# Where the softmax transposes, scores and value sums of two attentions stand between the weight products

## The reference, cut to what matters

```python
s = einsum('bgrqm', q, k) * SCALE - slopes * dist      # selected and window keys, 8 heads each
p = masked_softmax(s, mask)
o = einsum(p, v)
o_nsa = g[0] * o_cmp + g[1] * o_slc + g[2] * o_win     # o_cmp: 15 compressed keys
mixed = sigmoid(gate_a) * (o_nsa @ w_branch_a) + sigmoid(gate_b) * (z @ w_branch_b)
```

```python
s = einsum('bqhd,bqkhd->bhqk', q, k_sel) * HEAD_DIM_2 ** -0.5
out = einsum(softmax(where(valid, s, -inf)), v_sel)
```

## The kernel before, in words

| step | engine | work |
|---|---|---|
| a | TensorE | scores of both rows, 64-row operands in two halves of the array (`TT`), below S |
| a+1 to a+4 | VectorE, ScalarE | `biased`, `exps`, `factors`, `scale_p` (in `SM`; ScalarE at a+4) |
| a+4, a+5 | TensorE | three transposes of row 2n, then of 2n+1 (`turn`, line 433, into the one bank PB[6]), below T |
| a+5, a+6 | ScalarE | `copy_p` of each to `PT` |
| a+6 | TensorE | sums of values of both rows, 64-column outputs (`PT`,`QKV`), below V, and every second time those of the compressed keys (`PTC`,`KCV`), below C |
| a+7 | ScalarE, VectorE | every second time `make_o_hi`, `make_o_lo`, which free PB[7] |

## Time and profile before

### The profile page before, as it was taken

The page is one execution under the profiler, slowest core; times in us unless marked ns, Lnnn a source line. Parts: engine busy times, 40 slices in busy tenths (PEclk is TensorE's granted clock), DMA queues, the critical chain, the costliest instruction groups (busy, mean ns, idle before and its releaser), DMA issues.

```text
span 929.4 us, 14094 instructions
## 1 busy us (share of the span) xinstructions
PE 918.4 (99%) x5341; PEld 787.6 (85%) x5341; DVE 684.9 (74%) x1205; ACT 523.9 (56%) x899; POOL 15.2 (2%) x20
## 2 busy tenths in 40 slices
PE   8999999999999999999999999999999999999997
PEld 6899887788888888888899988888788888888886
DVE  5779976378776666678688989998786676666665
ACT  6656677745654544456544436654946664445443
POOL 0300000000000000000000000000000000000000
PEclk9999999999999999999999999999999999999999
DMA  9845454655565555554655844555475256655551
GB/s 334 307 146 159 137 150 127 237 200 186 166 207 196 193 193 189 193 190 147 206 173 151 235 134 154 172 175 178 138 236 176 93 163 219 217 189 182 181 182 46
DMA packets 89458, 168.54 MB, mean 181 GB/s; under 512 B 7536, under 2 KB 11952, under 8 KB 89136
## 3 DMA queue, kind: packets, MB, share of 16 engines
q1 hardware_dynamic: 89024, 167.13, 55.5%
q10 hardware_dynamic: 368, 0.52, 0.2%
HBM read 164.77 MB, written 1.05 MB: 178 GB/s over the span
## 4 chain that ended last, share of the span: by engine, by line
PE 94%; DVE 3%; issue 1%; DMA 1%; ACT 1%; SPq 0%; POOLq 0%; POOL 0%; DVEq 0%
PE pb L429 92%; PE pb L433 2%; DVE YC L1987 1%; DVE wlo L1527 1%; DMA raw<-in_w_in 1%; ACT whi L976 0%; DVE DG L1966 0%; DVE ST L1677 0%; DVE XS L2261 0%; ACT S L1461 0%; DVE SM L1672 0%; SPq L367 0%; DVE X L2254 0%; DVE ST L2209 0%; ACT SM L976 0%
## 5 line engine op out<-in xcount | busy, mean ns | idle before, releaser
L1527 DVE TENSOR_TENSOR wlo<-raw,whi 128x1024 fp32r<-128x1024 f32 (+2 forms) x300 | 356.0, 1212 | 118.0 <-ACT whi L976 117.4
L976 ACT ACTIVATE whi<-raw 128x1024 fp32r<-128x1024 f32 (+2 forms) x302 | 308.7, 1044 | 134.3 <-PE pb L429 122.2
L429 PE MATMUL pb<-XT,whi 128*128 128x256 f32 (+2 forms) x1424 | 311.1, 334 | 0.8 <-issue 0.8
L429 PEld LDWEIGHTS pb<-XT,whi 128*128 128x128 f32 (+1 forms) x1424 | 234.9, 190 | 23.7 <-issue 4.0
L429 PE MATMUL pb<-whi,ZO 128*128 128x512 f32 (+1 forms) x808 | 252.4, 389 | 0.0
L429 PE MATMUL pb<-XT,wlo 128*128 128x256 f32 (+1 forms) x1032 | 205.5, 282 | 0.0
L429 PE MATMUL pb<-whi,XT 128*128 128x512 f32 (+1 forms) x544 | 176.3, 395 | 2.3 <-ACT whi L976 2.3
L429 PEld LDWEIGHTS pb<-whi,ZO 128*128 128x128 f32 x808 | 151.3, 188 | 31.6 <-DVE wlo L1527 1.1
L429 PEld LDWEIGHTS pb<-XT,wlo 128*128 128x128 f32 (+1 forms) x1032 | 166.8, 190 | 9.6
L429 PE MATMUL pb<-wlo,ZO 128*128 128x512 f32 (+1 forms) x404 | 156.6, 388 | 0.0
L429 PEld LDWEIGHTS pb<-whi,XT 128*128 128x128 f32 x544 | 101.8, 189 | 23.9 <-ACT whi L976 2.8
(11 more groups left out here) (238 smaller groups left out, 593.2 us busy)
## 6 DMA issues: line engine op xcount, KB each, us to landing
raw<-in_w_in SPq DMA_DIRECT2D x107, 512.0 KB, 3.8
raw<-in_w_ff SPq DMA_DIRECT2D x64, 512.0 KB, 4.7
raw<-in_w_up SPq DMA_DIRECT2D x32, 512.0 KB, 4.5
raw<-in_w_down SPq DMA_DIRECT2D x32, 512.0 KB, 5.1
raw<-in_w_branch_b SPq DMA_DIRECT2D x8, 512.0 KB, 4.8
raw<-in_w_out SPq DMA_DIRECT2D x8, 512.0 KB, 4.7
raw<-in_wx_kv SPq DMA_DIRECT2D x8, 512.0 KB, 5.2
raw<-in_w_attn_out SPq DMA_DIRECT2D x8, 512.0 KB, 3.4
```

The lines of the kernel that those rows point to most:

```text
L429: return e.matmul(o, l, r, start=start, stop=stop, skip_group_check=True)
L976: return e.activation(o, i, ACT.Copy, scale=scale)
L1527: e.tensor_tensor(wlo[u % NW][:, 0:c], raw[u % NRAW][:, 0:c], whi[u % NW][:, 0:c].bitcast(F32), ALU.subtract).then_inc(lo, 1)
```

## The change

In the first attention the transposes of row 2n stand at a+3 and those of row 2n+1 at a+6 (a+5 for the last pair); the values of a pair stand at a+9 (a+8 for n = 6, a+6 for n = 7). Since `pair_at` goes in threes, gap s in `pair_at` now holds, in this order: T of the odd row of pair n-2, S of pair n, V of pair n-3, T of the even row of pair n-1. ScalarE's copies stand at the transposes' step +2 (even rows) and +1 (odd rows); `scale_p` stays at a+4. In the second attention the values of a head move from gap 29+2h to 30+2h, behind the scores and the transposes there.

```diff
+        values_of = {a + (9 if i < 6 else 8 if i == 6 else 6): i for i, a in enumerate(pair_at)}
+        def turn_step(j):
+            return pair_at[j // 2] + (3, 6 if j < 14 else 5)[j % 2]
...
+                    def turn_item(j):
+                        e.wait_ge(sc_p, j + 1)
+                        if j:
+                            e.wait_ge(pt_out, j)
+                        for c in range(3):
+                            i = turn(PB[6][:, c * P:c * P + P], SM[j % 4][:, c * P:c * P + P])
+                        i.then_inc(pt_done, 1)
+                    for j in range(1, 16, 2):
+                        if s == turn_step(j):
+                            turn_item(j)
                     if s in pair_of:
...
-                    for p in range(2):
-                        if s - 4 - p in pair_of:
...
-                    if s - 6 in pair_of:
-                        n = pair_of[s - 6]
+                    if s in values_of:
+                        n = values_of[s]
...
+                    for j in range(0, 16, 2):
+                        if s == turn_step(j):
+                            turn_item(j)
                     yield
...
-                    h = (s - 29) // 2
-                    if s % 2 == 1 and 0 <= h < 8:
+                    h = (s - 30) // 2
+                    if s % 2 == 0 and 0 <= h < 8:
                         e.wait_ge(pt_out, 16 + h + 1)
...
-                    for p in range(2):
-                        if s - 5 - p in pair_of:
-                            copy_p(2 * pair_of[s - 5 - p] + p, 0)
-                    if s - 7 in pair_of and pair_of[s - 7] % 2:
-                        f = pair_of[s - 7] // 2
+                    for j in range(16):
+                        if s == turn_step(j) + (2, 1)[j % 2]:
+                            copy_p(j, 0)
+                    if s - 1 in values_of and values_of[s - 1] % 2:
+                        f = values_of[s - 1] // 2
                         make_o_hi(f, 7, (pair_done, f + 1))
```

More of the change, by code:

```diff
@@ L1249, in attention2 @@
             def attention2():
-                for s in range(45):
+                for s in range(46):
                     if s == 1:
@@ L1266, in attention2 @@
                         copy_p((s - 29) // 2, 16)
-                    h = (s - 30) // 2
-                    if s % 2 == 0 and 0 <= h < 8:
+                    h = (s - 31) // 2
+                    if s % 2 == 1 and 0 <= h < 8:
                         make_o_hi(h, 6, (pv_done, 16 + h + 1))
```

## The result

| | runs | median us | range |
|---|---|---|---|
| before | 22 | 929.76 | 928.66 to 931.23 |
| changed | 22 | 931.10 | 930.51 to 931.62 |

The ratio is 1.0015 with a 95% interval of 1.0009 to 1.0021: the change costs 1.34 us, between 0.8 and 2.0. The forecast was 932.1, so 2.2 us; the direction was right and the size about six tenths of it. The result lies in the stated range of 929.9 to 933.4, but outside the forecast's own range of 931.6 to 932.9, and inside the 0.2% that I called about what a measurement can tell. In some sets a few executions are 1 to 1.7 us longer than the rest, most of them at a mean granted clock of 0.996 or 0.997 against 0.998 to 1.000, so the ratios, which are computed from all runs, can differ a little from the quotient of the medians.

The account below looks back on a forecast made before the run. TensorE was taken as the bound, busy 918.4 of 929.4 us. Losses of 1.55 + 0.36 + 0.27 = 2.18 us on 929.91 gave 932.1 us, own range 931.6 to 932.9, whole range 929.9 to 933.4.

Parts of the forecast that it names:

- The wait in gap 31: First attention, end of ga1: row 12's transposes wait for ScalarE's copies and scaling, 1.55 us slower.
- Row 1's hidden place: First attention: row 1's transposes leave gap 15, where a wait hid them, for gap 16, +0.36 us.
- everything up to the end of x1 is free: TensorE's work between gap 13 and the product after x1's bank wait costs nothing, even if row 0 waits.
- The lost pairing: First attention: values follow scores in five gaps instead of six, +0.27 us.
- Gap 28: One gap after ga0's end: row 10's transposes come about even with ScalarE; 0 taken, 0.2 us no surprise.
- The joining: Both attentions: side work stands in 22 gaps fewer, taken as worth 0 us.
- leaving and re-entering the weight products has a price: Rival: the product recorded 0.50 instead of 0.39 is real time, saved 22 times, 2.4 us; 929.7, chance 0.17.
- the 0.2% line: Whole kernel: slower by over 0.2% means above 931.8 us, chance 0.62; within 0.33, faster 0.05.
- my cases: Whole kernel: forecast 0.52, no gap 31 wait 0.12, price of returns 0.17, both 0.04, dearer transposes and more waits 0.15.

Follow-up runs that it names:

- e6_both_mended: Changed kernel with row 12's transposes in gap 32 and row 1's in gap 15; median 929.24 us, 0.9997 times the kernel before.
- e1_row12_later: Changed kernel with row 12's transposes alone in gap 32 instead of ending gap 31; median 929.55 us, 1.0001 times the kernel before.
- e4_first_only: Kernel before with only the first attention's part of the change; median 931.37 us, 1.0018 times the kernel before.

## Why the forecast came out as it did

**The wait in gap 31** was forecast as 1.55 us and recorded as 1.58 of idle time, and costs 1.63. ScalarE's list ended 3.81 us after the unit's last product (154.05 + 0.47 - 150.71) where the forecast had 3.83, and TensorE started 0.15 behind it instead of 0.06. The cause (ScalarE tied to ga1's tiles, then a list of four pieces) stood the test of two kernels that change it in different ways.

**Row 1's hidden place** was forecast as 0.36, measured as 0.41 together with row 2's short wait. The step that everything up to the end of x1 is free held exactly, 8.53 us in all three arrangements.

**The lost pairing** was forecast as 0.27. No run measures just this; the related readings give 0.30 and 0.20. By the estimate from the drain of about 175 ns in the Trainium skill (TensorE: Matmul & The Clock Gate, Single matmul latency) it would be 0.18, less than any of them; no run here isolates a drain.

**Gap 28** was left at 0 with a margin of nothing, and there was next to no wait: its even row's transposes start 0.61 us after C (142.37 - 141.76), in gap 34 0.58, and the list of waits from 60 to 190 us holds one for a copy, that of gap 31, and one for a scaling, that of row 0. Its nearness to a wait of some tenths makes this zero partly luck.

**The joining** is the term that was mis-sized. The prediction put it at nothing ("By the 0.01 above this is worth nothing"), from one comparison in the full array: S and T in one gap 1.03 against 1.04 apart. The runs show 0.18 for the second attention. For the first they leave what the changed kernel did not lose, with the forecast's 0.27 kept for the pairing: the wait's 1.63, the 0.41 and the 0.27 make 2.31, the distance grew by 1.63, so joining gave 0.68 for 15 gaps. By e6_both_mended and e1_row12_later it is 0.55 + 0.14 = 0.69. With 0.08 on the wait and 0.05 on row 1 the forecast of 2.18 becomes 2.18 + 0.13 - 0.68 - 0.18 = 1.45, the traces' sum. Two errors lay in the step. I read a difference of a hundredth from starts that are printed to a hundredth, and applied it 22 times. And I applied the price of T behind S to T behind V, where the trace had no row; a good part of the saving is there (0.12 in gap 25, with T behind V in the first attention too). The rival that leaving and re-entering the weight products has a price was thus right in sign: 0.03 to 0.05 for each gap in the mean, less than half of the 0.11 that it took from the recorded length of the product behind. As a whole it would have given no change, which the interval excludes.

**The size of the whole** was 2.18, only 0.3 above the 0.2% line, and the chances were 0.62 on its far side. The joining, 0.86 us in all that I took for nothing, put it on the near side. None of my cases had its middle at the measured 931.1: the range held it because it was drawn around all of them, and not because the main sum was close.

## What to carry to other kernels

Side work for an engine that is the bound costs its own length wherever it stands, so before moving a piece, look at what the old place hid (here a wait for a bank) and whose results it needs at the new place. A helper engine that runs ahead is ahead only until it must copy something the bounding engine has just finished; work that depends on the helper does not belong at the end of such a unit. When an effect is a few tenths of a microsecond, compare distances between fixed instructions inside the traces, in kernels with one edit each; whole spans and the 10 to 33 runs of each kernel taken here don't separate it.

## What the runs showed that I had not expected

The time that joining saves is real but small: 0.026 us for each gap in the full array, about 0.04 in the mean where a part of it is in the divided array (with 0.27 for the lost pairing), more where transposes stand behind values between products of 512 columns (0.12 in gap 25), nothing where they stand in front of scores (gap 31 of e1_row12_later). The recorded length of the product behind a gap (0.50 against 0.39) overstates it two to four times.

The start of the program moves by up to 2.1 us between profiles, all of it ahead of gap 13, with a wait for the first weights of 2.3 us before and 1.1 us with the change. In the two latest starts the granted clock also fell for some microseconds after this wait, to a mean of 0.59 (before) and 0.71 (e4_first_only) between 12 and 16 us; in e6_both_mended it stayed at 1.00 there after a wait of 2.0 us. Yet the medians of the runs of one kernel move by only 0.3 us between sets.
